# Sums of squares copied out of their PSUM bank, their roots ten steps later, and three VectorE operations moved, in the scan of a four-layer network

## The reference

```python
def ssd_mixer(hn, w_in, ..., d_skip, norm_g, w_out):
    z, xbc, dt_raw = split(hn @ w_in)
    xbc = silu(depthwise_conv(xbc));  xs, bm, cm = split(xbc)
    ...
    y = bidir_scan(qc, kb, v_f, v_b, log_a_f, log_a_b)   # 32 heads of 64, state 128, 4 groups
    y = y + xh * d_skip[..., None]                       # the skip sum
    y = y.reshape(s, 2048) * silu(z)                     # the gate
    yg = y.reshape(s, 4, 512)
    yg = yg * rsqrt(mean(yg * yg, -1) + EPS)             # a root per position and group
    return (yg.reshape(s, 2048) * norm_g) @ w_out
```

## Time and profile before

| what | value |
| --- | --- |
| median of 3 executions | 2641.96 us |
| profiled execution | 2640.6 us |
| its span | 2638.7 us |
| PE busy | 2606.3 us (99%) |
| DVE busy | 1527.8 us (58%) |
| ACT busy | 1176.7 us (45%) |
| POOL busy | 253.2 us (10%) |
| granted TensorE clock | 1.00 |

### The profile page before, as it was taken

One profiled execution on the slowest core, in us unless ns is written; L12 is line 12 of the kernel. 1 busy time (PEld: TensorE's weight loads), 2 busy tenths in 40 slices (PEclk: granted clock), 3 DMA queues, 4 the chain that ended last, 5 costly groups with the idle time before them and its releaser, 6 DMA issues.

```text
span 2638.7 us, 32995 instructions
## 1 busy us (share of the span) xinstructions
PE 2606.3 (99%) x11700; PEld 2023.5 (77%) x11700; DVE 1527.8 (58%) x2128; ACT 1176.7 (45%) x1854; POOL 253.2 (10%) x200
## 2 busy tenths in 40 slices
PE   9999999999999999999999999999999999999999
PEld 7854788888786557788888776788888777888887
DVE  4467677643988785677643787543333536533333
ACT  3326443333546894444333687532333425422332
POOL 0012100000103781100000230000000001000000
PEclk9999999999999999999999999999999999999999
DMA  5310333333244442233333220233333321333332
GB/s 210 96 56 1 105 100 96 95 96 95 82 136 122 126 128 79 81 97 97 100 97 96 94 64 1 79 98 98 98 95 96 104 80 51 94 96 97 98 100 96
DMA packets 71287, 245.97 MB, mean 93 GB/s; under 512 B 7420, under 2 KB 7548, under 8 KB 70816
## 3 DMA queue, kind: packets, MB, share of 16 engines
q1 hardware_dynamic: 70256, 236.43, 29.1%
q0 software_dynamic: 944, 8.40, 0.9%
HBM read 242.56 MB, written 2.24 MB: 93 GB/s over the span
## 4 chain that ended last, share of the span: by engine, by line
PE 92%; DVE 3%; ACT 3%; issue 1%; POOL 1%; DMA 0%; SPq 0%; DVEq 0%; ACTq 0%; POOLq 0%
PE bank L332 27%; PE bank L333 26%; PE bank L334 26%; PE bank L1694 1%; PE bank L880 1%; PE bank L534 1%; PE bank L519 1%; PE bank L911 1%; PE bank L520 1%; PE bank L900 1%; PE bank L2517 1%; DVE over_hn L700 1%; PE bank L1701 1%; PE bank L1133 0%; PE bank L683 0%
## 5 line engine op out<-in xcount | busy, mean ns | idle before, releaser
L322 DVE TENSOR_TENSOR wlo<-wraw,whi 128x1024 fp32r<-128x1024 f32 x409 | 509.2, 1246 | 577.6 <-ACT whi L299 576.9
L332 PE MATMUL bank<-hnhi,whi 128*128 128x512 f32 x1952 | 779.2, 399 | 2.0 <-DVE arena L1544 1.2
L333 PE MATMUL bank<-hnlo,whi 128*128 128x512 f32 x1952 | 760.6, 390 | 0.0
L334 PE MATMUL bank<-hnhi,wlo 128*128 128x512 f32 x1952 | 760.4, 390 | 0.0
L299 ACT ACTIVATE whi<-wraw 128x1024 fp32r<-128x1024 f32 x409 | 430.3, 1053 | 534.5 <-DMA wraw<-in_w 534.4
L332 PE MATMUL bank<-ahi,whi 128*128 128x512 f32 x1184 | 463.1, 391 | 1.0 <-DVE alo L555 0.7
L333 PE MATMUL bank<-alo,whi 128*128 128x512 f32 x1184 | 460.8, 389 | 0.0
L334 PE MATMUL bank<-ahi,wlo 128*128 128x512 f32 x1184 | 460.7, 389 | 0.0
L332 PEld LDWEIGHTS bank<-hnhi,whi 128*128 128x128 f32 x1952 | 366.4, 188 | 110.2 <-issue 34.3
L333 PEld LDWEIGHTS bank<-hnlo,whi 128*128 128x128 f32 x1952 | 366.6, 188 | 80.5 <-issue 6.5
L334 PEld LDWEIGHTS bank<-hnhi,wlo 128*128 128x128 f32 x1952 | 366.4, 188 | 77.5
(11 more groups left out here) (297 smaller groups left out, 2504.4 us busy)
## 6 DMA issues: line engine op xcount, KB each, us to landing
wraw<-in_w SPq DMA_DIRECT2D x410, 512.0 KB, 3.6
arena<-cs_scratch SPq DMA_DIRECT2D x20, 512.0 KB, 5.8
over_a<-cs_scratch SPq DMA_DIRECT2D x12, 512.0 KB, 6.2
arena<-in_rpb POOLq DMA_DIRECT2D x1, 2880.0 KB, 14.1
out_dram<-xT SPq DMA_DIRECT2D x8, 256.0 KB, 2.0
arena<-in_t_step POOLq DMA_DIRECT2D x2, 897.0 KB, 4.8
arena<-in_t_ab POOLq DMA_DIRECT2D x1, 1472.0 KB, 6.6
xT<-in_x SPq DMA_DIRECT2D x2, 512.0 KB, 6.6
```

Source lines behind the costliest of these rows:

```text
L322: dve.tensor_tensor(wlo[:, slot * BLOCK:(slot + 1) * BLOCK], wraw[:, slot * BLOCK:(slot + 1) * BLOCK], whi[:, slot * BLOCK:(slot + 1) * BL ...
L332: pe.matmul(out, wh, ah, start=start, stop=False)
L333: pe.matmul(out, wh, al, start=False, stop=False)
L334: return pe.matmul(out, wl, ah, start=False, stop=stop)
```

## The change

Four edits, all in the scan:

1. The roots of groups 0 and 1 are made in two parts. At q = 29 and 45 ACT only copies the sum out of bank 4 into the tile of the root (`summed`), and the root itself (table load, Ln, Exp) is made from that tile at q = 39 and 55. Groups 2 and 3 are as before.
2. `ssd_rstd` is counted twice per group, so `pe_turn` of the next group waits for the copy, and the scalings wait for the root.
3. `dve_gained(0)` and `(1)` move from q = 36 and 38 to q = 47 and 51.
4. `skip(14)` moves from behind `probs(61)` to behind `probs(63)` and the low part of y tile 0.

```diff
@@ pe_turn, pe_ssd_total, dve_gained, ssd_free
-                pe.wait_ge(sem("ssd_rstd"), g - 1)
+                pe.wait_ge(sem("ssd_rstd"), 2 * g - 3)
...
-                pe.wait_ge(sem("ssd_rstd"), 3)
+                pe.wait_ge(sem("ssd_rstd"), 6)
...
-            dve.wait_ge(sem("ssd_rstd"), j.quarter().value(1, 1))
+            dve.wait_ge(sem("ssd_rstd"), j.quarter().value(2, 2))
...
-                pe.wait_ge(sem("ssd_rstd"), 4)
+                pe.wait_ge(sem("ssd_rstd"), 8)
@@ act_ssd
+            def summed(g):
+
+                act.wait_ge(sem("ssd_sum"), g + 1)
+                act.activation(ssd_rs(At(4 * g)), bank[4][:, :], ACT.Copy).then_inc(sem("ssd_rstd"), 1)
+
             def group(g):
-                act.wait_ge(sem("ssd_sum"), g + 1)
+                if g < 2:
+                    act.wait_ge(sem("ssd_rstd"), 2 * g + 1)
+                else:
+                    act.wait_ge(sem("ssd_sum"), g + 1)
                 act_exp_ln(act)
-                act_rsqrt(act, bank[4][:, :], ssd_rs(At(4 * g)), 1.0 / SEQ, 4 * EPS, "ssd_rstd")
+                total, root = bank[4][:, :], ssd_rs(At(4 * g))
+                act_order(act, act.activation(root, root if g < 2 else total, ACT.Ln, bias=const(4 * EPS, 0, P), scale=1.0 / SEQ))
+                act.activation(root, root, ACT.Exp, scale=-0.5).then_inc(sem("ssd_rstd"), 1 if g < 2 else 2)
...
                 if q in (29, 45):
-                    group(q // 16 - 1)
+                    summed(q // 16 - 1)
+                if q in (39, 55):
+                    group(q // 16 - 2)
@@ dve_ssd
-                if q >= 5 and q % 4 == 1:
+                if q >= 5 and q % 4 == 1 and q < 61:
                     skip(q // 4 - 1)
...
-                if q in (36, 38):
-                    dve_gained(dve, At(q // 2 - 18))
+                if q in (47, 51):
+                    dve_gained(dve, At((q - 47) // 4))
             dve_low_part(dve, "c_out", At(0))
+            skip(14)
             skip(15)
```

## The result

The changed kernel is slower: 2647.07 us (2645.04 to 2649.70, 14 executions) against 2641.75 us (2640.05 to 2642.68, 14 executions), ratio 1.0021 with a 95% interval of 1.0013 to 1.0028. I had forecast 2644.9 us. A second set on another occasion gave 2645.01 against 2641.15 us, ratio 1.0015 (1.0006 to 1.0024). All 25 executions of the changed kernel have a median of 2645.84 us, so the change costs some 4 to 5 us, one and a half times my +2.9.

What follows compares the result with a forecast made beforehand. PE, busy 99% of the span, was taken as the bound, with at most about 3.6 us to win. Terms -1.3 - 0.7 + 3.0 + 1.9 = +2.9 us gave a median of 2644.9 us; 8-in-10 range 2641.0 to 2647.2 us.

Steps and rivals of the forecast that it cites:

- The 3.7 us of waits forecast for steps 60 to 63: Sign that the forecast is right: PE's waits on `probs` in steps 60 to 63 sum to some 3.7 us.
- Step 29, -1.3: Copy in place of a root at step 29: PE's wait of 1.30 us for ACT's copy of x goes, -1.3 us.
- Rival (e): PE's wait at step 29 stays, something other than the root holding the copy back: +1.3 on the forecast, 2646.2 us; 3%.
- Steps 36 to 40, -0.7: Scalings moved away, group 0's root at 39: 0.7 us won of PE's waits of 1.18 and 0.40 us.
- rival (c): ACT's new loads reach transposes at steps 44 to 47, POOL gives nothing back, gain at 937.99 fails: 2646.5 us; 12%.
- Steps 47 and 51, 0: Scalings add 0.74 us each on DVE; at 51 up to 0.7 us of PE delay, swallowed by the late root: nothing.
- Step 55, +3.0: Group 1's root and load, 3.8 us, fall where ACT has no slack before step 63: +3.0 us at scan's end.
- Rival (a): Late root absorbed by slack of DVE and PE at step 63: -2.0 to -2.7 us, 2639.3 to 2640.0 us; 10%.
- (d): A table change costs more than its row, ACT pausing 1.28 us behind each load: +2.6 us, 2647.5 us; 3%.
- Edit 4, +1.9: Late skip sum of pair 14 delays POOL's last squares, so PE's last sum over a group comes later: +1.9 us.
- Rival (b): Only the tail is covered, the last sum not late: +1.0 us, 2643.0 us; 15%.

Runs made afterwards that it cites:

- one_switch: Kernel before with group 0's sum copied at step 29, its root at 45, and group 1's root moved behind the loop: 2640.44 us, ratio 0.9995.
- early_alone: Kernel before with group 0's sum copied at step 29, its root at 39, and group 1's root moved behind the loop: 2640.61 us, ratio 0.9997.
- scaling_at_48: Changed kernel with the second scaling at step 48 instead of 51: 2645.24 us, ratio 1.0018.
- root1_at_45: Changed kernel with the whole root of group 1 back at step 45: 2647.98 us, ratio 1.0024.
- late_root_alone: Kernel before with only group 1's sum copied at step 45 and its root made at 55: 2645.60 us, ratio 1.0015.
- changed_again: Changed kernel measured once more, nothing altered: 2645.01 us, ratio 1.0015.
- before_again: Kernel before measured once more, nothing altered: 2640.85 us, ratio 1.0000.
- added_wait: Kernel before with six more chained ACT copies behind the last exponential, to delay PE once: 2647.20 us, ratio 1.0022.

## Why the prediction was wrong

The direction, the main new waits and what ends them were right. The sum was too small, by 1.4 us at full clock (+4.3 against +2.9), and in the first set of executions by 2.4 (+5.3). Of these 2.4 us some 0.5 are the gain that did not come at steps 36 to 40, 0.5 are edit 4, 0.5 lie outside the scan's three stretches, and the last 1.0 is what the first set lost to the clock beyond its share before. The 3.7 us of waits forecast for steps 60 to 63 were 2.3 there and 1.3 at step 52. PE's idle time in the 260 us was forecast as 6.8 us and is 7.9.

**Step 29, -1.3: right.** PE starts the second group of transposes without a wait, 1.4 to 1.5 us earlier beside value(0). Rival (e) falls.

**Steps 36 to 40, -0.7: too large a gain, measured -0.1 at step 40 and -0.2 by step 49.** This is the step of the prediction that failed in its mechanism. POOL was faster as forecast (its first two instructions behind 931 us take 1.06 us each, the first 1.60 us before) and PE's z product starts 0.6 us earlier beside the second transposes. But all but 0.1 us of it is lost again two steps on. I took the last exponential of step 40 as what holds `probs(40)`. DVE's order has the weight split of step 40 ahead of it, and that waits for ACT's half of the split, which stands behind the new root:

```profile
936.80 1.28 ACT L341 ACT_TABLE_LOAD   x1
938.09 0.72 ACT L1765 ACTIVATE arena<-arena,stats 128x512 f32<-128x512 f32 x1
938.85 0.63 ACT L1766 ACTIVATE arena<-arena 128x512 f32<-128x512 f32 x1
939.39 1.04 ACT L299 ACTIVATE whi<-wraw 128x1024 fp32r<-128x1024 f32 x1
```

```profile
940.46 2.09 DVE L322 TENSOR_TENSOR wlo<-wraw,whi 128x1024 fp32r<-128x1024 f32 x1 [0.67 <-ACT whi L299]
942.48 2.34 DVE L1829 TENSOR_TENSOR arena<-arena,bank 128x1024 f32<-128x1024 f32 x2
```

```profile
940.42 1.06 POOL L1623 TENSOR_TENSOR mT<-arena 128x512 f32<-128x512 f32 x1
```

The same two instructions before the change:

```profile
939.97 1.21 DVE L322 TENSOR_TENSOR wlo<-wraw,whi 128x1024 fp32r<-128x1024 f32 x1
...
940.03 2.06 POOL L1623 TENSOR_TENSOR mT<-arena 128x512 f32<-128x512 f32 x1
```

The split starts 0.03 us behind the end of ACT's half and takes 2.09 us instead of 1.21 us. POOL worked beside it before the change too; what is new is the order. Before, DVE's split started 0.06 us ahead of POOL's instruction, and POOL's took 2.06 us; now POOL's starts 0.04 us ahead and takes 1.06 us, and the split is the one that is stretched. `probs(40)` starts at 942.48, though the exponential it needs was ready at 941.75. With its 1.21 us the split would have ended at 941.67 (an estimate), and the exponential would have come last, as I had it: the wait for ACT matters because it put the split behind POOL. I had asked only for the operand of `probs(40)`, not for what stands ahead of it on its engine. That the root at step 39 is the cause, and not something else in the change, one_switch shows beside early_alone, which differs from it in the place of this root alone: without a root at 39 value(40) stands 1.0 us earlier and has no wait. The other fear, rival (c), that the root at 39 and the load before tanh reach the transposes at steps 44 to 47, did not come: PE has no wait there, and ACT waits for PE again at step 46 (0.33 us). That POOL gives nothing back at the end is the part of (c) that came.

**Steps 47 and 51, 0: right, for the reason given.** The wait of 1.27 us at step 52 was larger than my "up to 0.7", since the scaling took 1.07 and the split behind it 2.31 us beside POOL's additions. It was swallowed, as scaling_at_48 shows; without the late root, as in root1_at_45, it is not, and costs 1.4 us.

**Step 55, +3.0: right,** measured +3.1; alone, late_root_alone, +3.1 at full clock (one execution). Rival (a), the late root absorbed, falls. So does (d): no pause behind a load. The Trainium skill's 2.66 us for a switch (ScalarE: Activation LUTs, "What ACT_TABLE_LOAD costs") does not show in any of the loads above; its 1283 ns for the load itself does.

**Edit 4, +1.9: mis-sized, measured +2.4.** I took `added(13)` to be faster because no low part of DVE runs beside it. After the change `dve_low_part(1)` does, and both are stretched, 1.73 us and 1.34 us. It gained nothing, and that is the 0.45 us of the term. `gated(14)` starts 2.6 us later beside value(63), as forecast (2.5). Rival (b), a covered tail, falls.

**The clock: not in the sum.** I held it at 1.00 because the profile before did. Its share is not settled to better than 1 us: the median of 14 executions was 2.0 us above those at full clock, that of the next 11 only 0.1. What stays open is also 0.4 us between the waits (+3.8) and the executions at full clock (+4.3); between changed_again and before_again 0.1 us of it lies behind the last sum and 0.3 us ahead of the scan, where profiles without the stretch at 12 us differ by more than that from one another (831.02 to 832.15 us), whatever the kernel.

**The range.** The forecast's own range, 2643.7 to 2646.2 us, is not what the bounds of the terms add up to: from +0.3 to +4.6 us they give 2642.2 to 2646.6 us. The full-clock part of the change, +4.3 us, lies inside that, and the clock took the first set above it. The sum had no term for the clock.

## What to carry to other kernels

Work moved later on an engine that has no slack at the end of a loop is paid there, less only the waits that this engine still has on the way (3.8 us of root and load less a wait of 0.84 us here), however much room it leaves where it stood; before moving it, find the last moment at which that engine waits for the bound one and count what lies behind. For every wait that is to go, walk the whole queue ahead of the instruction, not only its operand. And where one table switch serves two uses, or a wait behind the loop can hold it, move it there: that was worth 2.0 to 2.3 us here, where the change cost 4.3.

## What the runs showed of the hardware

With a single wait of 2.96 us on PE no execution of eleven kept the full clock, and in the profiled one 3.4 us at half of TensorE's clock stand at that wait. So a wait can cost more than itself: added_wait lost 6.1 us in the median (2647.20 against 2641.15) where its stretch up to the last sum, without the half clock, would have lost some 2.7 us (an estimate, 11.66 - 7.28 - 1.7). Where DVE and POOL work side by side in these rows, the one that starts first keeps its time: DVE's weight split took 1.21 us where it started 0.06 us ahead of POOL's L1623 (2.06 us), and 2.09 us where it started 0.04 us behind it (1.06 us). At the end of the scan DVE's low part, started behind POOL's L1637, took 1.34 instead of 0.68 us, and POOL's L1644, started while that ran, 1.73 instead of 1.29 us.
